# The last up product on modulated rows from its fifth block on

## Chip, cores and metric

One core of one Trainium2 chip runs the whole program. The metric is the device time of one execution in microseconds; the kernel before has a median of 1041.04 us over three runs.

## The reference

Two blocks of layers run one after the other on 256 rows (tokens) of 1024 numbers, all float32. The change is in the last layer's feed-forward part, which computes, with `x` the residual stream after the mixer:

```
h2 = rmsnorm(x, norm2_g) * (1 + sc2) + sh2      # sc2, sh2: one number per feature
x  = x + g2 * (square(relu(h2 @ w_ff1)) @ w_ff2)  # w_ff1 1024 x 4096, w_ff2 4096 x 1024
```

The rmsnorm's factor is one number per token (the reciprocal root of the mean square), `norm2_g`, `1 + sc2` and `sh2` are one number per feature.

## The kernel before

Float32 products run as three products of a split: each operand is its high part (rounded to the matmul's float32r form) plus the rest, and high x high, high x low and low x high are summed in PSUM. Weights come as units of 128x1024 through a ring of four (`raw`, loaded by SyncE's queue). ScalarE writes the high part of unit c (`wH`, line L1361, helper `hi`), VectorE the low part (`wL = raw - wH`, L2187, helper `lo`), and TensorE reads both. `ahead(i, U)` prepares the two units that are four further on, so units 8 and 9 (block 4's) are prepared at block 2. High parts are also counted against the ring: unit c waits until TensorE has finished unit c - 4. SyncE's queue loads unit c + 4 when the low part of unit c is done.

The last up product ("ff1") has 16 blocks. A block is 256 of the 4096 features, that is two units, each with 8 slices of the contraction and 3 products a slice, 48 products in all. Weights are the stationary operand, the tokens (256 columns) the moving one. Blocks 0 to 3 are written out, 4 to 15 are a loop of four-block bodies on TensorE.

Before, the product starts before the row factors are known. The moving operand is `nH`, `nL` (gain times the residual, not yet scaled by the row factor), and `nH` carries two more columns, the high and low part of the shift `sh2`, so the products with `nH` have 258 columns and those with `nL` 256. For each block VectorE then adds up the two shift columns (`shift_out`, L3124), multiplies the rest by the row factor `rcol` from PSUM into a staging buffer (L3126), and frees the bank; ScalarE applies relu with the shift as bias (L1990); VectorE squares into `act_a` (L3116). There are two staging buffers. The row factor comes from GpSimd (a power of -1/2, L2014), goes through two diagonal matrices by VectorE (`rd`, L2366) and one product by TensorE after block 1 (L626), and VectorE copies it to `rcol` (L2372) before it reads block 0. Up to there the finished blocks wait in PSUM.

The earlier feature-major products ("qkv", "up0", "up1", L606 to L608) have the same loop form with 256 columns and without shift columns. GpSimd fetches tiles of the modulation weights with DMAs (L2030, `mod_fetch`), weights some rows, and computes roots. Each engine works through its queue in the order written.

Of the kernel before, what the change touches and what calls it, by code (L numbers as in the profile page):

```python
# [15 lines left out]
F32 = mybir.dt.float32  # L16
F32R = mybir.dt.float32r
ALU = mybir.AluOpType
# [3 lines left out]
P = 128  # L22
SEQ = 256
# [124 lines left out]
PRODS = {"down0": 0, "down1": 22}  # L148
ACTS = {"down0": 0, "down1": 22, "ff2": 44}
AUX = 4  # L150

# [49 lines left out]
def turns(eng, count, body, steps=None, each=0, between=None, before_last=None):  # L203


    head = count % 4 or 4
    for j in range(head):
        body(0, j)
    if between:
        between()  # L210
    n = (count - head) // 4
    tail = 4 if n == 1 or before_last else 0
    n -= tail // 4
    if n > 0:
        with eng.Fori(0, n) as i:
            if steps is None:
                for j in range(4):
                    body(i, head + j)
            else:
                with steps.loop(i, n, 4 * each):  # L220
                    for j in range(4):
                        body(i, head + j)
    for j in range(count - tail, count) if count > head else ():
        if before_last and j == count - 1:
            before_last()
        body(0, j)
# [6 lines left out]
def build(nc, a, out):  # L233
    with ExitStack() as ctx:
# [3 lines left out]
        def sem(name):  # L238
            return ctx.enter_context(nc.semaphore(name))
# [35 lines left out]
        def place(kib, *names):  # L275

            with ExitStack() as s:
                if kib:
                    sb(f"pad_{names[0][0]}", [P, int(kib * 256)], where=s)
                return [sb(*n, where=s) for n in names]  # L280
# [25 lines left out]
        hf, = place(16, ("hf", [P, TT, D]))  # L306
        xvd, = place(48, ("xvd", [P, KD, SEQ]))
        nH, nL, shift_out = place(56.1875, ("nH", [P, KD, 320], F32R), ("nL", [P, KD, SEQ], F32R), ("shift_out", [P, 2, 2]))
        zL, = place(0, ("zL", [P, KD, SEQ], F32R))
        zH = yH  # L310

# [80 lines left out]
        half_done = sem("half_done")  # L392
        shift_hi = sem("shift_hi")
        relu_done = sem("relu_done")
        fin_rows = sem("fin_rows")
        fin_act = sem("fin_act")
        fin_pool = sem("fin_pool")
# [100 lines left out]
        def U(name):  # L498
            return 2 * BLOCKS[name][0]
# [101 lines left out]
        def _(pe):  # L601
# [706 lines left out]
            def shifted_up():  # L1308

                def weights(i, c):  # L1310
                    return [y.rearrange("p (k n) -> p k n", k=KD) for y in w_unit(i, 8, c)]

                def tile(o, w, k):
                    mm(o[:, 0:SEQ + 2], w[0][:, k], nH[:, k, 0:SEQ + 2], start=k == 0, stop=False, skip_group_check=True)  # L1314
                    mm(o[:, 0:SEQ], w[0][:, k], nL[:, k], start=False, stop=False, skip_group_check=True)  # L1315
                    return mm(o[:, 0:SEQ + 2], w[1][:, k], nH[:, k, 0:SEQ + 2], start=False, stop=k == KD - 1,  # L1316
                              skip_group_check=True)

                def body(i, j):
                    if j == 3:  # L1320
                        pe.wait_ge(r_done, r_order.index("ff1") + 1)
                    o = (bank("ff1", i, j), ps[AUX + (BANK["ff1"] + j) % 4])
                    if isinstance(i, int) and j == 0:
                        w = [weights(i, U("ff1") + f) for f in range(2)]
                        for k in range(KD):
                            if k == 3:
                                pe.wait_ge(unstaged, STAGED["wo_c"] + 4)
                                turn_pair(3, AUX + 3)
                            if k % 2 == 0:
                                pe.wait_ge(x_ready, READY["n2"] + k // 2 + 1)  # L1330
                            for f in range(2):
                                last = tile(o[f], w[f], k)
                                if k == KD - 1:
                                    last.then_inc(unit_done, 1)
                    else:
                        for f in range(2):
                            w = weights(i, U("ff1") + 2 * j + f)
                            for k in range(KD):
                                last = tile(o[f], w, k)
                            last.then_inc(unit_done, 1)  # L1340
                    if isinstance(i, int) and j == 1:
                        row_scale("ff1")
                turns(pe, BLOCKS["ff1"][1], body)
            mixer_out([zH, zL])
            shifted_up()
            down("ff2", FF2_TILES)
# [3 lines left out]
        def _(act):  # L1350
# [12 lines left out]
            def ahead(i, c):  # L1363

                hi(i, 8, c + SPLIT)
                hi(i, 8, c + SPLIT + 1)
# [46 lines left out]
            def projected(name):  # L1413

                def part(j):
                    act.wait_ge(unstaged, STAGED[name] + j + 1)
                    for t in range(TT):
                        c = slice(j * 256, (j + 1) * 256)
                        q = fn(hf[:, t, c], h[:, t, c], ACT.Square, accum_out=sqp[:, t, j:j + 1])
                        if j == 3:  # L1420
                            q.then_inc(sq_done, 1)

                def pair(b):
                    turned_pair("n2", "n2", b, AUX + b, lambda k: gs2[:, k:k + 1], nH[:, :, 0:SEQ])
                for j in range(4):
                    if j == 2:
                        part(0)
                        fn(nH[:, :, SEQ:SEQ + 1], modc[:, 24:32, 0].unsqueeze(2),
                           ACT.Copy).then_inc(shift_hi, 1)
                        pair(0)  # L1430
                    if j < 3:
                        act.wait_ge(unit_done, U(name) + OUT_DONE[j])
                        act.wait_ge(unstaged, STAGED[name] + j - 1)
                        fn(stage[:, (STAGED[name] + j) % 2].rearrange("p a b -> p (a b)"), ps[(BANK[name] + j) % 4][:],
                           ACT.Copy).then_inc(bank_free, 1)
                        ahead(0, U(name) + 2 * j)
                    else:
                        pair(1)
                        part(1)
                        part(2)  # L1440
                        ahead(0, U(name) + 2 * j)
                        pair(2)
                        pair(3)
                        part(3)
# [536 lines left out]

            win_act()
            projected("wo_c")
            def rectified(i, j):
                ahead(i, U("ff1") + 2 * j)
                n = STAGED["ff1"] + j
                act.wait_ge(bank_free, i * 4 + (BANK["ff1"] + j + 1))
                for f in range(2):
                    s = stage[:, n % 2, f]
                    last = fn(s, s, ACT.Relu, bias=shift_out[:, n % 2, f:f + 1])  # L1990
                last.then_inc(relu_done, 1)
# [20 lines left out]
        def _(pool):  # L2012
# [6 lines left out]
            def norm(n):  # L2019
                pool.wait_ge(ms_done, STAT[n] + 1)  # L2020
                inverse_root(rstd[:], msq[:]).then_inc(rstd_done, 1)
# [127 lines left out]
            pool.wait_ge(pw_in, 8)  # L2149
            inverse_root(st_r[:, 3, 4:8], st_r[:, 2, 4:8]).then_inc(pw_out, 1)  # L2150
            norm("n2")
            pool.wait_ge(m_o, RET_H)
            mod_fetch(64, MOD_TILES)
            gate_store(1)
# [13 lines left out]
        def _(dve):  # L2168
# [941 lines left out]
            ahead(0, U("ff1"))  # L3110
            row_scale("ff1")

            def square(i, j):
                dve.wait_ge(relu_done, i * 4 + (j + 1))
                s = stage[:, (STAGED["ff1"] + j) % 2]
                tt(act_a[:, bass.ds((i * 4 + j) * 2, 2)], s, s, ALU.mult).then_inc(unstaged, 1)  # L3116

            def up_scaled(i, j):
                n = STAGED["ff1"] + j
                dve.wait_ge(unit_done, i * 8 + (U("ff1") + 2 * j + 2))  # L3120
                dve.wait_ge(unstaged, i * 4 + (n - 1))
                b = [ps[x + (BANK["ff1"] + j) % 4] for x in (0, AUX)]
                for f in range(2):
                    nc.vector.tensor_reduce(shift_out[:, n % 2, f:f + 1], b[f][:, SEQ:SEQ + 2], AX, ALU.add)  # L3124
                for f in range(2):
                    last = tt(stage[:, n % 2, f], b[f][:, 0:SEQ], rcol[:], ALU.mult)  # L3126
                last.then_inc(bank_free, 1)
                if not (isinstance(i, int) and j == 0):
                    ahead(i, U("ff1") + 2 * j)
                    square(i, j - 1)  # L3130
            turns(dve, BLOCKS["ff1"][1], up_scaled, st, 0, before_last=first_tiles("ff2"))
            square(0, BLOCKS["ff1"][1] - 1)

# [112 lines left out]
```

## Time and profile before

| | |
|---|---|
| median of three runs | 1041.04 us (1038.68 to 1042.88) |
| span of the profiled execution | 1037.3 us |
| profiled execution's own time | not listed apart from its span |
| TensorE busy | 96% of the span |
| VectorE, ScalarE, GpSimd busy | 82%, 59%, 10% |
| last up product | 847 to 939 us of the span |

Rows give the start in us, the length in us, engine, line, operation, what is written and read, and a count; square brackets hold the engine's idle time ahead of the instruction and what ended it. TensorE's matmuls overlap, so the distance between starts is what counts there. A length of VectorE or GpSimd includes the time in which an instruction was held up after it was issued.

### The profile page before, as it was taken

The page shows a single profiled execution, that of the slowest core. Times are in us where ns is not written, and L with a number is a line of the kernel's source. Part 1 is how long each engine was busy: PE and PEld are TensorE (multiplying, and loading weights), DVE is VectorE, ACT ScalarE, POOL GpSimd, SP SyncE. Part 2 cuts the span into 40 slices and gives each one's busy share as a digit, 9 for nine tenths or more (in the row PEclk, how much of TensorE's full clock was granted, in tenths as well). Part 3 has the DMA queues.
Part 4 walks back from the last instruction along what each step waited for, and adds up shares of the span by engine and source line. Part 5 has one row for each costly group of instructions (what it writes and reads, how often), then busy time and mean ns, then how long its engine had stood idle before and what let it go on. Part 6 is the DMA issues. An engine that isn't in the chain of part 4 may idle for free.

```text
span 1037.3 us, 20795 instructions
## 1 busy us (share of the span) xinstructions
PE 998.8 (96%) x7662; PEld 926.7 (89%) x7662; DVE 848.9 (82%) x1566; ACT 608.4 (59%) x1056; POOL 102.2 (10%) x115
## 2 busy tenths in 40 slices
PE   6999999999999999999899999999998899999996
PEld 6999898999998889988899998898777799998884
DVE  5899978798889979887898999867788876668856
ACT  6687534666666464574676666456364565545443
POOL 1014522000000000001100001001200210000001
PEclk9999999999999999999999999999999999999998
DMA  9674323687776868837786657834412158766852
GB/s 290 178 223 135 103 64 101 204 228 219 222 210 218 287 175 256 278 100 262 252 237 197 186 185 251 283 95 130 152 62 82 41 152 245 193 188 219 278 152 115
DMA packets 216194, 193.09 MB, mean 186 GB/s; under 512 B 6032, under 2 KB 193568, under 8 KB 216000
## 3 DMA queue, kind: packets, MB, share of 16 engines
q1 hardware_dynamic: 206560, 158.09, 51.4%
q0 software_dynamic: 9136, 33.51, 9.5%
q8 instruction: 41, 0.67, 0.3%
q10 hardware_dynamic: 432, 0.61, 0.2%
q14 instruction: 25, 0.20, 0.1%
HBM read 191.14 MB, written 1.06 MB: 185 GB/s over the span
## 4 chain that ended last, share of the span: by engine, by line
PE 84%; DVE 8%; ACT 4%; DMA 2%; issue 1%; POOL 1%; POOLq 0%; ACTq 0%; DVEq 0%
PE ps L606 23%; PE ps L607 22%; PE ps L608 22%; PE ps L1315 3%; PE ps L1316 3%; PE ps L1314 3%; DVE wL L2187 2%; DMA modw<-in_w_mod_t 1%; PE ps L887 1%; PE ps L874 1%; ACT wH L1361 1%; PE ps L1144 1%; DVE cv L2209 1%; PE ps L829 1%; PE ps L783 1%
## 5 line engine op out<-in xcount | busy, mean ns | idle before, releaser
L1361 ACT ACTIVATE wH<-raw 128x1024 fp32r<-128x1024 f32 x298 | 312.9, 1061 | 254.9 <-PE ps L608 190.7
L2187 DVE TENSOR_TENSOR wL<-raw,wH 128x1024 fp32r<-128x1024 f32 x298 | 357.7, 1225 | 59.5 <-ACT wH L1361 58.8
L606 PE MATMUL ps<-yH,wH 128*128 128x256 f32 x704 | 195.7, 278 | 3.7 <-DVE wL L2187 3.6
L607 PE MATMUL ps<-yL,wH 128*128 128x256 f32 x704 | 194.5, 276 | 0.0
L608 PE MATMUL ps<-yH,wL 128*128 128x256 f32 x704 | 194.5, 276 | 0.0
L606 PEld LDWEIGHTS ps<-yH,wH 128*128 128x128 f32 x704 | 132.2, 188 | 4.7 <-DVE wL L2187 1.5
L607 PEld LDWEIGHTS ps<-yL,wH 128*128 128x128 f32 x704 | 132.2, 188 | 0.1
L608 PEld LDWEIGHTS ps<-yH,wL 128*128 128x128 f32 x704 | 132.2, 188 | 0.0
L606 PE MATMUL ps<-wH,aH 128*128 128x512 f32 (+1 forms) x308 | 119.4, 388 | 0.0
L608 PE MATMUL ps<-wH,aL 128*128 128x512 f32 (+1 forms) x308 | 119.0, 386 | 0.0
L607 PE MATMUL ps<-wL,aH 128*128 128x512 f32 (+1 forms) x308 | 119.0, 386 | 0.0
L606 PE MATMUL ps<-wH,xH 128*128 128x256 f32 (+1 forms) x304 | 94.2, 310 | 3.3 <-DVE xL L2187 2.3
L607 PE MATMUL ps<-wL,xH 128*128 128x256 f32 (+1 forms) x304 | 91.9, 302 | 0.0
L608 PE MATMUL ps<-wH,xL 128*128 128x256 f32 (+1 forms) x304 | 91.9, 302 | 0.0
L3038 DVE SCALAR_TENSOR_TENSOR cv<-stage,cols,cv 128x254 f32<-128x254 f32 (+1 forms) x176 | 73.1, 477 | 0.0
L1315 PE MATMUL ps<-nL,wH 128*128 128x256 f32 x256 | 72.5, 283 | 0.0
L606 PE MATMUL ps<-xH,wH 128*128 128x256 f32 x256 | 71.5, 279 | 1.0 <-DVE xL L2240 0.8
L1314 PE MATMUL ps<-nH,wH 128*128 128x258 f32 x256 | 72.3, 282 | 0.0
L2030 POOL DMA_DIRECT2D modw<-in_w_mod_t x48 | 26.4, 551 | 464.5 <-DVE modc L2209 406.4
L1316 PE MATMUL ps<-nH,wL 128*128 128x258 f32 x256 | 72.1, 282 | 0.0
L608 PE MATMUL ps<-xH,wL 128*128 128x256 f32 x256 | 70.9, 277 | 0.0
L607 PE MATMUL ps<-xL,wH 128*128 128x256 f32 x256 | 70.9, 277 | 0.0
(430 smaller groups left out, 2178.2 us busy)
## 6 DMA issues: line engine op xcount, KB each, us to landing
raw<-in_f_w_up SPq DMA_DIRECT2D x88, 512.0 KB, 4.9
raw<-in_w_ff SPq DMA_DIRECT2D x64, 512.0 KB, 4.5
modw<-in_w_mod_t POOLq DMA_DIRECT2D x48, 512.0 KB, 5.5
raw<-in_f_w_down SPq DMA_DIRECT2D x44, 512.0 KB, 4.6
raw<-in_a_w_in SPq DMA_DIRECT2D x32, 512.0 KB, 4.9
raw<-in_w_in SPq DMA_DIRECT2D x22, 512.0 KB, 4.3
raw<-in_w_kv SPq DMA_DIRECT2D x16, 512.0 KB, 5.2
raw<-in_a_w_out SPq DMA_DIRECT2D x8, 512.0 KB, 3.4
```

Source lines behind the costliest of these rows:

```text
L606: mm(o, l[0], r[0], start=first, stop=False, skip_group_check=check)
L607: mm(o, l[0], r[1], start=False, stop=False, skip_group_check=check)
L608: return mm(o, l[1], r[0], start=False, stop=last, skip_group_check=check)
L783: tr = nc.tensor.transpose(ps[first + k // 2][:, o:o + P], rows[:, t, k * P:(k + 1) * P], ident)
L829: last = mm(ps[AUX + g][:, x * P:(x + 1) * P], feat[:, 8 + h0 + x, t * P:(t + 1) * P], feat[:, f0 + h0 + x, t * P:(t + 1) * P], start=True ...
L1314: mm(o[:, 0:SEQ + 2], w[0][:, k], nH[:, k, 0:SEQ + 2], start=k == 0, stop=False, skip_group_check=True)
L1315: mm(o[:, 0:SEQ], w[0][:, k], nL[:, k], start=False, stop=False, skip_group_check=True)
L1316: return mm(o[:, 0:SEQ + 2], w[1][:, k], nH[:, k, 0:SEQ + 2], start=False, stop=k == KD - 1, skip_group_check=True)
L1361: fn(slot(wH, c), raw[:, c % RAW], ACT.Copy).then_inc(hi_done, 1)
L2030: pool.dma_start(mod_tile(m), a["w_mod_t"][m * P:(m + 1) * P, :]).then_inc(mod_in[m % MOD_RING], 16)
L2187: return tt(o, x, hi.bitcast(F32), ALU.subtract)
L3038: c = stt(o[:, d:], x[:, 0:SEQ - d], w, o[:, d:], ALU.mult, ALU.add)
```

## The change

From block 4 on (`SHIFTED_UP = 4`) the up product reads fully modulated rows `xH`, `xL` = norm2(x) scaled by row factor and gain, plus the shift. GpSimd adds `nH + nL` into `mt` (two instructions of 128x1024), multiplies by the row factor after `rcol` is there (two more), and its tile fetches follow behind. ScalarE adds the shift and rounds into `xH` (eight of 128x256) in its turn of block 2, between the high parts and relu 2. VectorE forms `xL` (eight of 128x256) behind square 1 in its turn of block 2. TensorE waits for both halves before the loop of blocks 4 to 15. In these blocks both units go into the two halves of one bank, ScalarE takes relu of the whole bank into the staging buffer ahead of its high parts, and VectorE only squares.

```diff
+SHIFTED_UP = 4
+        mt, = place(47.9375, ("mt", [P, KD, SEQ]))
 # TensorE
                 def body(i, j):
+                    if j >= SHIFTED_UP:
+                        modulated(i, j)
+                        return
...
+                def modulated(i, j):
+                    b = bank("ff1", i, j)
+                    for f in range(2):
+                        w = weights(i, U("ff1") + 2 * j + f)
+                        for k in range(KD):
+                            last = three(b[:, f * SEQ:(f + 1) * SEQ], [y[:, k] for y in w], [y[:, k] for y in X],
+                                         k == 0, k == KD - 1)
+                        last.then_inc(unit_done, 1)
+                turns(pe, BLOCKS["ff1"][1], body, between=lambda: pe.wait_ge(mt_ready, 2))
 # ScalarE
+            def modulated_hi():
+                for part in range(2):
+                    act.wait_ge(mt_rows, part + 1)
+                    for k in range(4 * part, 4 * part + 4):
+                        last = fn(xH[:, k], mt[:, k], ACT.Identity, bias=modc[:, 24 + k, 0:1])
+                    last.then_inc(mt_hi, 1)
             def rectified(i, j):
+                n = STAGED["ff1"] + j
+                if j >= SHIFTED_UP:
+                    act.wait_ge(unit_done, i * 8 + (U("ff1") + 2 * j + 2))
+                    act.wait_ge(unstaged, i * 4 + (n - 1))
+                    fn(stage[:, n % 2].rearrange("p a b -> p (a b)"), ps[(BANK["ff1"] + j) % 4][:],
+                       ACT.Relu).then_inc(bank_free, 1)
+                    ahead(i, U("ff1") + 2 * j)
+                    return
                 ahead(i, U("ff1") + 2 * j)
+                if j == 2:
+                    modulated_hi()
 # GpSimd, behind norm("n2") and ahead of mod_fetch(64, MOD_TILES)
+            for part in range(2):
+                c = slice(4 * part, 4 * part + 4)
+                pool.wait_ge(x_ready, READY["n2"] + 2 * part + 2)
+                ptt(mt[:, c], nH[:, c, 0:SEQ].bitcast(F32), nL[:, c].bitcast(F32), ALU.add).then_inc(mt_sum, 1)
+            pool.wait_ge(r_done, r_order.index("ff1") + 1)
+            for part in range(2):
+                c = slice(4 * part, 4 * part + 4)
+                pool.wait_ge(mt_sum, part + 1)
+                ptt(mt[:, c], mt[:, c], four_of(rcol), ALU.mult).then_inc(mt_rows, 1)
 # VectorE
+            def modulated_lo():
+                for part in range(2):
+                    dve.wait_ge(mt_hi, part + 1)
+                    for k in range(4 * part, 4 * part + 4):
+                        last = stt(xL[:, k], mt[:, k], modc[:, 24 + k, 0:1], xH[:, k].bitcast(F32), ALU.add, ALU.subtract)
+                    last.then_inc(mt_ready, 1)
             def square(i, j):
-                dve.wait_ge(relu_done, i * 4 + (j + 1))
+                if j < SHIFTED_UP:
+                    dve.wait_ge(relu_done, j + 1)
+                if j >= SHIFTED_UP - 1:
+                    dve.wait_ge(bank_free, i * 4 + (BANK["ff1"] + j + 1))
...
             def up_scaled(i, j):
                 n = STAGED["ff1"] + j
+                if j >= SHIFTED_UP:
+                    ahead(i, U("ff1") + 2 * j)
+                    square(i, j - 1)
+                    return
...
+                if j == 2:
+                    modulated_lo()
```

## Rows read from the trace of the kernel before

**Rows 1.** The page: span, busy shares, granted clock in 40 slices, chain by engine

```profile
span 1037.3 us, 20795 instructions
...
PE 998.8 (96%) x7662; PEld 926.7 (89%) x7662; DVE 848.9 (82%) x1566; ACT 608.4 (59%) x1056; POOL 102.2 (10%) x115
...
PEclk9999999999999999999999999999999999999998
...
PE 84%; DVE 8%; ACT 4%; DMA 2%; issue 1%; POOL 1%; POOLq 0%; ACTq 0%; DVEq 0%
```

**Rows 2.** Writers of PSUM by line, ns min/median/max, first and last start

```profile
L1314 PE MATMUL ps<-nH,wH x256: 278/283/470, 847.0 to 939.0; 128*128 128x258 f32 x128
```

**Rows 3.** Timeline of VectorE: its first read of finished blocks, both up products

```profile
542.39 0.69 DVE L3025 TENSOR_TENSOR stage<-ps,rd 128x512 f32<-128x512 f32 x1 [0.56 <-PE ps L608]
...
596.79 0.69 DVE L3025 TENSOR_TENSOR stage<-ps,rd 128x512 f32<-128x512 f32 x1 [0.57 <-PE ps L608]
...
871.07 0.23 DVE L3124 TENSOR_REDUCE shift_out<-ps 128x1 f32<-128x2 f32 x2 [1.34 <-PE ps L1316]
...
933.84 0.23 DVE L3124 TENSOR_REDUCE shift_out<-ps 128x1 f32<-128x2 f32 x2 [1.95 <-PE ps L1316]
```

**Rows 4.** Timeline of TensorE behind a stall of "qkv" and one of "up1"

```profile
15.62 0.39 PE L606 MATMUL ps<-xH,wH 128*128 128x256 f32 x1 [0.16 <-DVE wL L2187]
15.85 0.28 PE L607 MATMUL ps<-xL,wH 128*128 128x256 f32 x1
...
28.92 0.28 PE L607 MATMUL ps<-xL,wH 128*128 128x256 f32 x1
...
514.78 0.38 PE L606 MATMUL ps<-yH,wH 128*128 128x256 f32 x1 [1.33 <-DVE wL L2187]
```

**Rows 5.** Timeline of ScalarE and VectorE, 853 to 866 us

```profile
853.68 0.58 DVE L2366 TENSOR_SCALAR rd<-cst,rstd 128x128 f32<-128x128 f32 x2 [0.59 <-POOL rstd L2014]
854.29 2.36 DVE L2187 TENSOR_TENSOR wL<-raw,wH 128x1024 fp32r<-128x1024 f32 x2
859.63 0.42 DVE L2372 COPY rd<-ps 128x256 f32<-128x256 f32 x1 [2.98 <-PE ps L626]
...
861.02 0.91 ACT L1990 ACTIVATE stage<-stage,shift_out 128x256 f32<-128x256 f32 x2 [5.81 <-DVE stage L3126]
...
862.91 2.36 DVE L2187 TENSOR_TENSOR wL<-raw,wH 128x1024 fp32r<-128x1024 f32 x2 [1.13 <-ACT wH L1361]
```

**Rows 6.** Timeline of GpSimd: its longer instructions, the last root, the fetches

```profile
123.80 3.75 POOL L2089 TENSOR_TENSOR tok<-tok,sm 128x1024 f32<-128x1024 f32 x2 [10.57 <-DVE AT L2505]
127.51 5.64 POOL L2094 TENSOR_TENSOR zs<-zs,rows_a 128x1024 f32<-128x1024 f32 x2
151.02 2.02 POOL L2097 TENSOR_TENSOR tok<-tok,sm 128x1024 f32<-128x1024 f32 x1 [2.91 <-ACT tok L1538]
...
852.05 1.60 POOL L2014 TENSOR_TENSOR rstd<-msq,mhalf 128x2 f32<-128x2 f32 x1 [27.93 <-DVE msq L2360]
853.61 1.68 POOL L2030 DMA_DIRECT2D modw<-in_w_mod_t  x3
...
1023.18 1.29 POOL L2161 TENSOR_TENSOR hf<-h,rows_f 128x512 f32<-128x512 f32 x1 [16.53 <-DVE h L3143]
```

**Rows 7.** VectorE beside GpSimd (timeline), and its scalar-tensor-tensor by line

```profile
150.06 4.06 DVE L2187 TENSOR_TENSOR wL<-raw,wH 128x1024 fp32r<-128x1024 f32 x2
...
820.62 0.68 DVE L2829 TENSOR_TENSOR rope<-o_r 128x512 f32<-128x512 f32 x1
...
1022.34 0.69 DVE L3143 TENSOR_TENSOR h<-h,stage 128x512 f32<-128x512 f32 x1
...
1023.66 1.35 DVE L3143 TENSOR_TENSOR h<-h,stage 128x512 f32<-128x512 f32 x1
...
L3038 DVE SCALAR_TENSOR_TENSOR cv<-stage,cols,cv x176: 469/477/486, 208.2 to 623.2; 128x255 f32<-128x255 f32 x88, 128x254 f32<-128x254 f32 x88
```

**Rows 8.** Weight units, 846 to 875 us: DMA from issue to landing

```profile
DMA to landing us min/median/max: 4.1/4.8/8.8
```

More of the change, by code:

```diff
@@ L394, in build @@
         relu_done = sem("relu_done")
+        mt_sum = sem("mt_sum")
+        mt_rows = sem("mt_rows")
+        mt_hi = sem("mt_hi")
+        mt_ready = sem("mt_ready")
         fin_rows = sem("fin_rows")
@@ L1342, in body @@
                         row_scale("ff1")
-                turns(pe, BLOCKS["ff1"][1], body)
+                def modulated(i, j):
[7 more added lines that the diff above has]
+                turns(pe, BLOCKS["ff1"][1], body, between=lambda: pe.wait_ge(mt_ready, 2))
             mixer_out([zH, zL])
@@ L1983, in _ @@
             projected("wo_c")
-            def rectified(i, j):
+            def modulated_hi():
[4 more added lines that the diff above has]
+                    last.then_inc(mt_hi, 1)
+            def rectified(i, j):
+                n = STAGED["ff1"] + j
[6 more added lines that the diff above has]
+                    return
                 ahead(i, U("ff1") + 2 * j)
-                n = STAGED["ff1"] + j
+                if j == 2:
+                    modulated_hi()
                 act.wait_ge(bank_free, i * 4 + (BANK["ff1"] + j + 1))
```

## The prediction

> **What bounds the kernel now.** I read the busy shares first, then the chain of work that ended last, then the stretch of the last up product in order of time, and last every place where GpSimd ran beside VectorE. TensorE is busy 96% of the span at full clock (2.4 GHz throughout), and the chain lies on it for 84% [rows 1]. The last up product (16 blocks of 48 products, block 0 from 847.0 us) is such a stretch: no wait of TensorE shows between 847 and 939 us, its three product lines run without a break [rows 2]. So only two things can move the end: the time of a product in blocks 4 to 15, and a wait that TensorE gets. VectorE and ScalarE matter only where TensorE waits for them, and of that there is little room: in blocks 0 to 3 VectorE is the late one. It finishes the low part of block 3's first weights at 862.91 + 1.2 = 864.1 us, block 3 begins at about 865.2 (a block is 5.71 us, and block 3's end releases VectorE at 871.07) [rows 3, 5].
>
> **What a product costs.** VectorE's first read of each finished block marks the period: 871.07 to 933.84 us are eleven blocks, 5.71 us each, 118.9 ns a product (products of 258, 256 and 258 columns in turn) [rows 3]. The other feature-major up product, all 256 columns, has 542.39 to 596.79 us for ten blocks: 5.44 us, 113.3 ns [rows 3]. But 256 columns alone don't promise that: in the very first product of this form TensorE came out of a stall at 15.62 us, and from 15.85 to 28.92 it ran 111 products at 117.7 ns; after another stall, which ended at 514.78, came the very blocks that have the 5.44 us [rows 3, 4]. So there are two paces for the same product: the quick one would give 12 x (5.706 - 5.44) = 3.2 us, the slow one (117.7 ns, 5.65 us a block) 12 x 0.056 = 0.7 us. I take the quick one: it holds through the 54 us of a loop of the same form and length, the slow one through 13 us outside a loop; but block 4 will come out of a stall, so both stay in the range.
> The Trainium skill (TensorE: Matmul & The Clock Gate, step-by-step: what each phase is for) has one column streamed in each cycle, so that two columns fewer in 2 of 3 products would be worth 384 x 2 / 2.4 GHz = 0.3 us. By that rule the sum below would be +5.9 us. The rows differ: 118.9 ns are 285 cycles for 257 columns on average.
>
> **What is added, and where it lies.** Removed: VectorE's two small sums and two scalings (0.9 us a block) and ScalarE's two relus (0.9 us) in twelve blocks, replaced by one relu of 512 columns (no row has it; at most the 0.9 us of the two of 256) [rows 5]. In blocks 4 to 15 neither engine is on the path: per block ScalarE has 0.9 + 2.1 us, and its work ends 3.0 us after the block, the low parts of the weights at 4.2, the square at 4.9, all under 5.44. Worth nothing, cover 0.5 us; the weights' high part now waits for the block's end, which is hidden while block j + 2 is what they feed.
> Added on the path are the modulated rows: GpSimd two sums and two products of 128x1024, ScalarE eight 128x256, VectorE eight 128x256, and TensorE's wait for the last before block 4.
> *Prices.* GpSimd: 1.29 us for 128x512 with two full operands, so 2.6 us each (bounds: 1.9 us, a 128x1024 product by one number a row, and 2.8 us, one by a repeated row) [rows 6]. VectorE: a scalar-tensor-tensor is 0.48 us, back to back 0.39, so eight take 3.2 us [rows 7]. ScalarE: two 128x256 take 0.91, so eight 3.4 us [rows 5].
> *Contention.* The trace has GpSimd and VectorE holding each other up. A VectorE sum that takes 0.69 us took 1.35 when it began inside a GpSimd product (1023.18 to 1024.47), and two weight subtractions took 4.06 us in place of 2.35 around a 2.02 us GpSimd product [rows 5 to 7]. So an instruction of one with two SBUF inputs waits for the other's to end, and they take turns. I charge it so.
>
> **The chain of blocks 2 to 4, on the trace's clock.** GpSimd ends the root at 853.65, and the first sum follows at once (before, DMA issues stood there).
> 1. VectorE's diagonals (853.68) take turns with the sums: sum, diagonal, sum end at about 859.3; only then come the low parts of block 2's weights, which in the trace ran from 854.29: 859.3 to 860.5 and to 861.65. Block 2 wants its first at 859.4 and starts at 860.55: **+1.15 us**.
> 2. The row scale is copied behind them, at 862.0 in place of 860.05. GpSimd's two products run 862.05 to 867.15. VectorE's scalings read PSUM and one SBUF tile and pass. ScalarE: relu 863.0, high parts 863.8 to 865.8. VectorE's low part for block 3 is ready at 864.9, where the second product has just begun; it runs 867.15 to 868.35. Block 3 wants it at 866.25, starts at 868.4: **+2.15 us**.
> 3. VectorE's queue now is: low part 869.5, square 870.1, scalings of block 2 at 870.95, low parts 872.05 and 873.2, square 873.8, then the eight new ones to 876.95. ScalarE's eight are done at 871.8 (it held back relu 2, whose reader, the square, comes later still), so they cost nothing; the rows are VectorE's queue. Block 4 wants them at 868.4 + 5.7 = 874.1, starts at 877.0: **+2.9 us**.
> Sum: 6.2 us later into block 4, and nothing behind gives it back, since TensorE is the bound to the end. With 1.9 us a GpSimd instruction the same steps give 3.6, with 2.8 us 7.25. With no contention at all, 2.0 us are left: the eight new ones queued behind square 1 at 869.7 end at 872.9, block 4 wanted 870.9.
> Moved as well: GpSimd's three tile fetches go from 853.61 to 867.2 [rows 6]. Their readers are in the down product after 939 us, GpSimd's next step waits there anyway, and a weight transfer held up by them (unit 10 of the product, issued at 868.4, wanted by VectorE from 877.7) has 9 us against 4.8 in the median and 8.8 at worst [rows 8]. Nothing. TensorE's queue behind its new wait holds only its own products; the DMA queue's issues follow the low parts and shift with them.
> Net: +6.2 - 3.2 = **+3.0 us**. The profiled execution has a span of 1037.3 us [rows 1], 3.7 under the median of 1041.04, which I take to lie around it in both kernels: span 1040.3, time **1044.0 us** (+0.3%). Half a per cent, 5.2 us, is about what the timing can tell from no change.
>
> **Rivals.**
> - *Slow pace after the stall* (slower): block 4 starts from a wait and TensorE falls into the 117.7 ns pace and keeps it through the loop: 6.2 - 0.7 = +5.5, 1046.5 us, +0.53%. It decides from a pace of about 117 ns on. For it: the stretch from 15.62 us. Against: the one from 514.78, and the length of the quick stretch [rows 3, 4]. Chance 0.20.
> - *The time goes by columns alone* (slower): 118.9 ns for 257.3 columns on average leave 118.3 for 256, a gain of 0.35 us in all: 6.2 - 0.35 = +5.9, 1046.9 us. For it: it is what shortening a product does if the two paces have another cause; against: the 113.3 ns of the same shape. Chance 0.07. It is the rule of the Trainium skill's page named above.
> - *Little contention* (first sums before the weights, or shorter GpSimd instructions): delay 2.0 to 3.6, so 1039.8 to 1041.4 us, no change. For it: a VectorE product that took its plain 0.68 us at 820.62, in the midst of two GpSimd products [rows 7]. Against: the two disturbed rows above. Chance 0.22.
> - *Longer hold-up* (2.8 us and more a piece, or a turn lost): 7.25 - 3.2 = +4.1 at the quick pace, 1045.1; with the slow one 1047.6. Chance 0.11.
> - *The stage buffers become the bound*: ScalarE's relu of block j waits for the square of j - 2. At 4.9 of 5.44 us it doesn't; if each block lost 0.27 us, the gain would be gone: 1047.2. Chance 0.03.
> My forecast itself 0.37. A gain of over 5.2 us has no source: with no delay whatever it is 3.2 us, 1037.8.
>
> **Numbers.** Range 1039.5 to 1047.3 us: from no contention at the quick pace to the slow pace with the stall as worked out. The likeliest alone: 1042.5 to 1045.5. Slower by over 0.5% are most of the slow-pace cases and the last: 0.21. Faster by over 0.5%: 0.02. Same: 0.77.
>
> **What would show it.** VectorE's low part of block 2's weights after 859 us; waits of TensorE before blocks 2, 3 and 4 of about 1, 2 and 3 us, the last put down to VectorE's write of xL; GpSimd's products over by 867 us; the period of blocks 5 to 15 at 5.44 (or 5.65) us. I am wrong if GpSimd's four take turns otherwise with VectorE (then the waits differ), or if the new period is still 5.7 us.

## The result and the profile after

The changed kernel takes 1044.52 us in the median of 20 runs (1040.39 to 1050.41), the kernel before 1040.58 (20 runs, 1038.47 to 1046.74). The ratio is 1.0037, 95% interval 1.0022 to 1.0051: slower by 3.9 us (2.3 to 5.3). That is clear of the noise, but below the half per cent from which the prediction counts a change. Forecast were 1044.0 us and "same".

Page of the changed kernel: span, busy shares, granted clock in 40 slices.

```profile
span 1044.5 us, 20752 instructions
...
PE 1001.9 (96%) x7662; PEld 929.2 (89%) x7662; DVE 847.9 (81%) x1526; ACT 606.5 (58%) x1052; POOL 111.7 (11%) x119
...
PEclk9999989999999999999999999999999999999998
```

Set beside [rows 1], the span is 7.2 us longer, and 3.9 us of that are not the change: the last up product starts at 850.90 in place of 847.01 us, and none of the added instructions has run by then (a second execution of the same program, in experiment 7, starts it at 847.88). A stretch of short products at 129 to 155 us had a mean granted clock of 0.87 here and 0.93 before; the "8" in the row of the clock is that stretch. So from here on each trace is read from the start of its up product, and **its length to the first product of the down stage** is the measure: 92.34 us before (847.01 to 939.35), 96.09 after (850.90 to 946.99), +3.75 us. Behind it the kernels need 97.95 us before and 97.51 after. The timing of the whole says +3.9.

**The waits.** TensorE's waits in the changed kernel, 850 to 946 us (TensorE's line, the writer that it waited for: us in total, times, longest), and its products around the starts of blocks 2 and 3, in time:

```profile
PE ps L612 <- DVE xL L3161: 3.0, 1, 3.0
PE ps L1320 <- DVE wL L2230: 1.5, 1, 1.5
```
```profile
862.90 0.59 PE L632 MATMUL ps<-rd,cst 128*128 128x256 f32 x2
863.63 0.36 PE L1320 MATMUL ps<-nH,wH 128*128 128x258 f32 x1
...
869.31 0.28 PE L1322 MATMUL ps<-nH,wL 128*128 128x258 f32 x1
871.06 0.36 PE L1320 MATMUL ps<-nH,wH 128*128 128x258 f32 x1 [1.46 <-DVE wL L2230]
```

Before, TensorE had no such wait [rows 2]. Block 2 starts behind the two row-scale products (L632) and is too little late for the view of waits to list it. I count a delay from start to start, less what the same step takes without a wait: block 3 is +1.63 us late (1.75 less 0.12), block 4 +3.14 (876.74 to 880.00, 3.26 less 0.12). Block 2 is about +0.4 late: its second product starts 12.92 us behind the product's start, 12.54 before. That makes 5.2 us.

**Who made them.** GpSimd, then VectorE, then ScalarE of the changed kernel in order of time; a length includes the time in which an instruction was held up.

```profile
857.52 2.40 POOL L2189 TENSOR_TENSOR mt<-nH,nL 128x1024 f32<-128x1024 f32 x1
859.88 2.39 POOL L2189 TENSOR_TENSOR mt<-nH,nL 128x1024 f32<-128x1024 f32 x1
865.03 4.80 POOL L2194 TENSOR_TENSOR mt<-mt,rd 128x1024 f32<-128x1024 f32 x2 [2.77 <-DVE rd L2415]
869.74 1.69 POOL L2064 DMA_DIRECT2D modw<-in_w_mod_t  x3
```
```profile
857.58 2.42 DVE L2409 TENSOR_SCALAR rd<-cst,rstd 128x128 f32<-128x128 f32 x1 [0.59 <-POOL rstd L2048]
859.92 2.42 DVE L2409 TENSOR_SCALAR rd<-cst,rstd 128x128 f32<-128x128 f32 x1
...
865.13 0.74 DVE L3184 TENSOR_TENSOR stage<-ps,rd 128x256 f32<-128x256 f32 x2
...
867.80 4.25 DVE L2230 TENSOR_TENSOR wL<-raw,wH 128x1024 fp32r<-128x1024 f32 x2 [1.13 <-ACT wH L1378]
...
876.42 3.25 DVE L3161 SCALAR_TENSOR_TENSOR xL<-mt,modc,xH 128x256 fp32r<-128x256 f32 x8
```
```profile
871.31 3.30 ACT L2006 ACTIVATE xH<-mt,modc 128x256 fp32r<-128x256 f32 x8
...
878.35 1.06 ACT L1378 ACTIVATE wH<-raw 128x1024 fp32r<-128x1024 f32 x1 [2.95 <-DMA raw<-in_w_ff]
...
892.87 0.60 ACT L2014 ACTIVATE stage<-ps 128x512 f32<-128x512 f32 x1 [2.94 <-PE ps L614]
...
941.75 0.60 ACT L2014 ACTIVATE stage<-ps 128x512 f32<-128x512 f32 x1 [2.95 <-PE ps L614]
```

VectorE's two diagonals take 0.58 us together in [rows 5]. Here the first is issued 0.06 us behind GpSimd's first sum and ends 0.08 us behind its end; the second does the same with the second sum (ends at 862.34 and 862.27): one is held up by one sum, 4.8 us together. Its two low parts for block 3, 2.36 us in [rows 5], take 4.25: the first is issued at 867.80, while GpSimd's second product runs, the product ends at 869.83, and block 3 starts at 871.06. The scalings of block 0 (L3184), which read PSUM and one tile of SBUF, stand inside the first of GpSimd's two products and take their plain 0.74 us for two: they pass, as assumed. VectorE then goes through the queue that the prediction lists: low part, square, scalings, low parts, square, and the eight of L3161 to 879.67; block 4 starts at 880.00. ScalarE waits 2.95 us for weights at 878.35, and 0.76 once more at 880.17, where before it had 0.7 us of such waits in the whole product; TensorE doesn't wait for it. The relu of a whole bank (0.60 us) shows the period of the last blocks: 892.87 to 941.75 are nine, 5.43 us each, against 5.71 us [rows 3].

**What nobody had forecast.** TensorE behind the wait for `xL`, first each product, then four stretches of the same time (columns: us, busy time and count of PE, PEld, DVE, ACT, POOL, granted clock, DMA share, GB/s):

```profile
880.00 0.58 PE L612 MATMUL ps<-xH,wH 128*128 128x256 f32 x1 [2.98 <-DVE xL L3161]
880.38 0.41 PE L613 MATMUL ps<-xL,wH 128*128 128x256 f32 x1
...
883.15 0.40 PE L614 MATMUL ps<-xH,wL 128*128 128x256 f32 x1
...
883.98 0.28 PE L614 MATMUL ps<-xH,wL 128*128 128x256 f32 x1
884.09 0.28 PE L612 MATMUL ps<-xH,wH 128*128 128x256 f32 x1
```
```profile
874.00:879.00 5.00, 3.02 (x26) 2.81 (x24) 5.00 (x10) 2.05 (x5) 0.00 (x0) 1.00 1.09 342
879.00:881.00 2.00, 0.99 (x4) 1.00 (x5) 2.00 (x7) 1.24 (x2) 0.00 (x0) 0.75 1.20 292
881.00:883.00 2.00, 2.00 (x12) 2.00 (x11) 2.00 (x3) 1.02 (x3) 0.00 (x0) 0.50 1.14 276
...
890.00:946.00 56.00, 56.00 (x497) 56.00 (x496) 31.31 (x33) 26.18 (x34) 0.00 (x0) 1.00 0.67 189
```

The first products start 213 ns apart, from 883.5 on 113: TensorE came out of the wait at 1.2 GHz (clock 0.50) and ran 15 products so. From 880.00 to 883.51 it started 16 products, 3.51 us where 113.3 ns each make 1.81: 1.7 us lost. Of that 0.1 us is lost at full clock too (0.22 us from the first product to the second in experiments 3 and 5), so 1.6 us are the clock's. The terms close: 5.2 + 1.7 - 3.2 = +3.7 us, measured +3.75.

### The profile page after: what moved, and what is told of

The parts are those of the page before. It is cut to its first block, busy times and chain, and to the rows that moved or that the text cites. A ratio compares the mean times of both kernels' runs of the same rounds, so it can differ in the third digit from the quotient of the medians.

```text
span 1044.5 us, 20752 instructions
## 1 busy us (share of the span) xinstructions
PE 1001.9 (96%) x7662; PEld 929.2 (89%) x7662; DVE 847.9 (81%) x1526; ACT 606.5 (58%) x1052; POOL 111.7 (11%) x119
## 4 chain that ended last, share of the span: by engine, by line
PE 77%; DVE 13%; ACT 4%; DMA 2%; issue 2%; POOL 1%; POOLq 0%; ACTq 0%; DVEq 0%
PE ps L612 23%; PE ps L613 23%; PE ps L614 23%; DVE wL L2230 3%; DMA modw<-in_w_mod_t 2%; PE ps L893 1%; ACT wH L1378 1%; PE ps L1150 1%; DVE cv L2252 1%; PE ps L880 1%; PE ps L789 1%; PE ps L1000 1%; DVE cv L3031 1%; DVE st_p L2791 0%; DVE modw L2252 0%
## 5 line engine op out<-in xcount | busy, mean ns | idle before, releaser
L612 PE MATMUL ps<-xH,wH 128*128 128x256 f32 x448 | 126.6, 283 | 3.8 <-DVE xL L3161 3.0
L613 PE MATMUL ps<-xL,wH 128*128 128x256 f32 x448 | 126.0, 281 | 0.0
L614 PE MATMUL ps<-xH,wL 128*128 128x256 f32 x448 | 126.0, 281 | 0.0
L612 PEld LDWEIGHTS ps<-xH,wH 128*128 128x128 f32 x448 | 86.1, 192 | 4.5 <-issue 4.4
L614 PEld LDWEIGHTS ps<-xH,wL 128*128 128x128 f32 x448 | 86.1, 192 | 0.0
L613 PEld LDWEIGHTS ps<-xL,wH 128*128 128x128 f32 x448 | 85.8, 191 | 0.0
```

The lines of the kernel that those rows point to most:

```text
L612: mm(o, l[0], r[0], start=first, stop=False, skip_group_check=check)
L613: mm(o, l[0], r[1], start=False, stop=False, skip_group_check=check)
L614: return mm(o, l[1], r[0], start=False, stop=last, skip_group_check=check)
```

## The experiments

"Product" is the length defined above, in a trace of the kernel ("traced again" is a second execution of the same program, "fill" means idle products ahead of the wait); the timed ratio is to the kernel before, run beside it.

| kernel | product | against before | timed ratio, 95% interval | pace from block 4 on |
|---|---|---|---|---|
| before | 92.34 us | | | 118.9 ns |
| after | 96.09 | +3.75 | 1.0037, 1.0022 to 1.0051 | 113.3 |
| after, traced again | 97.35 | +5.01 | not timed | 113.3 |
| 256 columns alone | 89.13 | -3.21 | 0.9957, 0.9937 to 0.9977 | 113.3 |
| GpSimd's four alone | 94.40 | +2.06 | 1.0001, 0.9984 to 1.0019 | 118.8 |
| 24 products fill the wait | 94.50 | +2.16 | 1.0017, 0.9996 to 1.0037 | 113.3 |
| half of xL | 95.45 | +3.11 | 1.0001, 0.9981 to 1.0021 | 117.7 |
| half of xL, traced again | 95.46 | +3.12 | not timed | 117.8 |
| half of xL, 12 fill | 95.44 | +3.10 | not timed | 117.8 |
| all of xL, 12 fill | 97.05 | +4.71 | not timed | 117.7 |
| without the sums | 95.10 | +2.76 | 1.0052, 1.0027 to 1.0076 | 113.3 |
| without the sums, traced again | 95.15 | +2.81 | not timed | 113.3 |
| modulated rows from block 8 | 90.20 | -2.14 | 0.9975, 0.9955 to 0.9996 | 118.8, from block 8 on 113.3 |

The two measures don't agree everywhere. A product length is that of one execution and leaves out what lies ahead of the product and behind it; the start of the product alone lies between 846.2 and 856.4 us in the thirteen traces. For GpSimd's four alone (+0.20% by the product) and half of `xL` (+0.30%) the product's figure lies above the timed interval, and the kernel without sums (+0.27%) is timed at +0.52%. So the product lengths show what happens inside the product, and no more.

**1. The columns alone.** The kernel before, with products of 256 columns from block 4 on; the shift is left out there.

```diff
-    mm(o[:, 0:SEQ + 2], w[0][:, k], nH[:, k, 0:SEQ + 2], ...)
+    mm(o[:, 0:n], w[0][:, k], nH[:, k, 0:n], ...)        # both products with nH
-    last = tile(o[f], w, k)
+    last = tile(o[f], w, k, SEQ + 2 if j < 4 else SEQ)
```

> The kernel before with one part alone: blocks 4 to 15 read nH with 256 columns instead of 258, and the shift is left out of these blocks (no shift sums by VectorE there, and the relu's bias is an old one). Theory A, the two columns alone cost the 0.27 us a block: the period of blocks 5 to 15 is 5.44 us as in the changed kernel, 3.2 us less in all, ratio to before about 0.997. Rival, the place or stride of nH in SBUF is the cause and xH, xL are what helped: the period stays 5.7 us, and the time is that of before. Second rival, a product's time goes by its columns: 0.03 us a block, 0.35 us in all.

Measured: no wait of TensorE in the product, which takes 3.21 us less; the kernel is faster, 1037.33 us against 1040.71. VectorE's first reads of finished blocks, in time:

```profile
886.24 0.75 DVE L3126 TENSOR_TENSOR stage<-ps,rd 128x256 f32<-128x256 f32 x2 [1.80 <-PE ps L1316]
...
918.88 0.76 DVE L3126 TENSOR_TENSOR stage<-ps,rd 128x256 f32<-128x256 f32 x2 [1.81 <-PE ps L1316]
```

Six blocks in 32.64 us, 5.44 each. The two columns are what costs; neither the operand nor the bank that the products go to does. VectorE's small sums over the two columns are gone here as well, but they aren't it: in the kernel before, TensorE's products from 854.61 to 858.89 us are 118.9 ns apart, and the first such sum runs at 860.09.

**2. GpSimd's four alone.** The kernel before with GpSimd's sums and products, and nobody that reads `mt`.

```diff
+    ptt(mt[:, c], nH[:, c, 0:SEQ].bitcast(F32), nL[:, c].bitcast(F32), ALU.add).then_inc(mt_sum, 1)
...
+    ptt(mt[:, c], mt[:, c], four_of(rcol), ALU.mult).then_inc(mt_rows, 1)
```

> The kernel before plus GpSimd's four new instructions alone (their result is read by nobody; its tile fetches follow them as in the changed kernel). Theory A, they hold up VectorE: the diagonals and the low parts of block 2's weights come 4 us late, low parts of block 3's 2.4 us late, TensorE waits about 0.4 us before block 2 and 1.5 us before block 3, none before block 4 (there VectorE has caught up), clock full: +1.9 us, ratio about 1.002. Rival, the waits of blocks 2 and 3 come from the moved fetches or from chance: VectorE's lengths stay 1.22 and 0.29 us and no wait shows, ratio 1.000.

TensorE's waits, then VectorE's diagonals and its low parts for block 3:

```profile
PE ps L1317 <- DVE wL L2199: 1.6, 2, 1.4
```
```profile
854.57 4.77 DVE L2378 TENSOR_SCALAR rd<-cst,rstd 128x128 f32<-128x128 f32 x2 [0.59 <-POOL rstd L2017]
...
864.78 4.23 DVE L2199 TENSOR_TENSOR wL<-raw,wH 128x1024 fp32r<-128x1024 f32 x2 [1.13 <-ACT wH L1364]
```

The delays of blocks 2 and 3 are there to 0.02 us (gaps of 0.75 and 1.73 us against 0.73 and 1.75 in the changed kernel), 2.06 us in all, and the product has no other delay. They are GpSimd's hold on VectorE, with VectorE's lengths as in the changed kernel; the moved fetches, the rival, are issued only at 866.74 us, when GpSimd's products are over. In this execution TensorE waited another 0.9 us late in the down product, behind a weight transfer of 12 us; that lies outside the product. The timing (+0.2 us, interval -1.7 to +2.0) does not confirm the 2.06 us.

**3. The wait filled.** Ahead of its wait TensorE runs 24 idle products of block 4's first weights into the bank that block 4 then starts anew.

```diff
+    def filled():
+        b, w = bank("ff1", 0, 4), weights(0, U("ff1") + 8)
+        for n in range(24):
+            mm(b[:, 0:SEQ], w[0][:, n % KD], nH[:, n % KD, 0:SEQ], start=n == 0, stop=n == 23, ...)
+        pe.wait_ge(mt_ready, 2)
-    turns(pe, BLOCKS["ff1"][1], body, between=lambda: pe.wait_ge(mt_ready, 2))
+    turns(pe, BLOCKS["ff1"][1], body, between=filled)
```

> The changed kernel, and TensorE runs 24 idle products (256 columns, block 4's first weights with nH, overwritten by block 4) ahead of its wait for xL; the values are those of the changed kernel. They take 2.8 us and fit into the wait of 3.0 us. Theory A, the fall of the granted clock to 0.5 for 3.4 us behind the wait comes from TensorE's idling there: the clock stays 1.00, block 4 takes 5.4 instead of 7.4 us, the time from the start of the last up product to the end is 1.6 us shorter than in the changed kernel, ratio to before about 1.002. Rival, the fall comes from something else near 880 us (the burst of transfers at 342 GB/s, the power drawn): it stays, and block 4 still takes 7 us.

Its wait for `xL` and a stretch behind block 4's start (849.93 + 29.10 = 879.03 us):

```profile
PE ps L612 <- DVE xL L3168: 0.3, 1, 0.3
```
```profile
880.00:882.00 2.00, 2.00 (x20) 2.00 (x20) 2.00 (x3) 0.92 (x3) 0.00 (x0) 1.00 1.04 255
```

Block 4 starts as late as in the changed kernel (29.1 us behind the product's start in both), the clock stays at 1.00, and the product is 1.59 us shorter. That is the price of the clock, against 1.6 from the rows above. The rival, the burst of transfers, falls too: it is still there (255 GB/s in this row, where the changed kernel has 276 to 292).

**4. Half of xL.** Four of VectorE's eight instructions are left out; the other half of `xL` keeps old contents. It ran twice.

```diff
-                    for k in range(4 * part, 4 * part + 4):
+                    for k in range(4 * part, 4 * part + 2):
```

> The changed kernel with four of VectorE's eight instructions for xL left out (the other half of xL keeps old contents). Theory A, block 4 waits for VectorE's queue: the wait before block 4 falls by 1.6 us, from 3.0 to 1.4; whether the clock still falls behind a wait of 1.4 us is open (in the trace of before waits of up to 1.3 us at 514 us did not show a lower clock): if it stays, block 4 is another 1.6 us shorter, 3.2 us in all, ratio to before about 1.000. Rival, the wait is for ScalarE's rows or GpSimd's products: it stays at 3.0 us.

> The kernel with four of the eight xL instructions left out, unchanged, one more look. If kernel and waits fix the pace, it is the slow one again (95.4 us from the product's start to the down product, clock 1.00 throughout). If it is chance, the quick one may come: 93.0 us.

The wait for `xL`, and the relu of two blocks six apart (first kernel):

```profile
PE ps L612 <- DVE xL L3161: 1.4, 1, 1.4
```
```profile
885.40 0.60 ACT L2014 ACTIVATE stage<-ps 128x512 f32<-128x512 f32 x1 [3.15 <-PE ps L614]
...
919.32 0.60 ACT L2014 ACTIVATE stage<-ps 128x512 f32<-128x512 f32 x1 [3.16 <-PE ps L614]
```

The wait shrinks by what was left out and the clock stays at 1.00, but a block takes 33.92 / 6 = 5.65 us: the slow pace of the prediction's first rival, both times. What the clock and the shorter wait give (3.2 us), the pace takes back (12 x 0.21 = 2.5): the product is 0.64 us shorter than in the changed kernel. The timing, 1.0001, is what was expected with the quick pace; why it is lower than the product length says stays open.

**5. What chooses the pace?** Two kernels with 12 products ahead of the wait, with half and with all of `xL`.

```diff
-        for n in range(24):
+        for n in range(12):
```

> As the half-xL kernel (four of VectorE's eight left out, so half of xL holds old contents), with 12 idle products of block 4's first weights ahead of the wait, 12 x 113 ns = 1.4 us, which is all of that kernel's wait. It asks what chose the slow pace of 117.7 ns there. Theory A (an idle wait at full clock is what puts TensorE on the slow pace): no wait is left, so blocks 4 to 15 run at 113.3 ns (period 5.44 us) and the product takes 95.46 - 12 x 0.21 = 92.9 us. Rival B (it is the shorter VectorE work, or where block 4 starts against the other engines): the slow pace stays, 117.7 ns, and the product takes 95.4 us.

> The changed kernel with 12 instead of 24 idle products ahead of its wait: 1.4 us of the 3.0 are filled, 1.6 are left idle. Theory A (idle at full clock without a fall of the clock gives the slow pace): if the clock stays at 1.00, blocks 4 to 15 run at 117.7 ns and the product takes 94.5 + 12 x 0.21 = 97.0 us. If the clock falls for this wait too, 113.3 ns come back and 1.6 us and more are lost to the clock, about 96.1. Rival B (the pace has nothing to do with the wait): full clock and 113.3 ns, 94.5 us.

TensorE's waits, with half and with all of `xL`:

```profile
PE ps L1320 <- DVE wL L2237: 1.5, 1, 1.5
```
```profile
PE ps L1320 <- DVE wL L2237: 1.6, 2, 1.5
PE ps L612 <- DVE xL L3168: 1.6, 1, 1.6
```

The second met theory A (clock 1.00, 117.7 ns, 97.05 us against the 97.0 expected). The first refutes it: no wait is left ahead of block 4, and the slow pace is there all the same. The rival fell too: in the second kernel VectorE has all its work and block 4 starts where it does in experiment 3, which runs at 113.3. So neither an idle wait nor the moment of the start sets the pace by itself.

**6. Without the sums.** GpSimd's two sums are left out, so `xH` and `xL` are made from `nH` alone. It ran twice.

```diff
-    ptt(mt[:, c], nH[:, c, 0:SEQ].bitcast(F32), nL[:, c].bitcast(F32), ALU.add).then_inc(mt_sum, 1)
...
-    ptt(mt[:, c], mt[:, c], four_of(rcol), ALU.mult).then_inc(mt_rows, 1)
+    ptt(mt[:, c], nH[:, c, 0:SEQ].bitcast(F32), four_of(rcol), ALU.mult).then_inc(mt_rows, 1)
```

> The changed kernel with GpSimd's two sums left out: its two products multiply nH alone (the low half nL is left out of the modulated rows). Theory A, the sums alone delay the diagonals and block 2's weights and through them the row scale: low parts of block 2's weights back at 2.2 us behind the root, no wait before block 2; the row scale is 1.0 us earlier, the products too, so the wait before block 3 stays near 1.2 to 1.6 us (the low part still meets the second product) and that before block 4 near 3. Delay 0.4 to 0.8 us less than in the changed kernel. Rival: it is the number of GpSimd pieces that counts, then half of all delays goes.

> The kernel without GpSimd's two sums once more (xH and xL made from nH alone), since its times and its one trace disagree: 1046.1 us in the median, but a product of only 95.1 us, 1.0 less than in the changed kernel, in the execution that was also its fastest. If the product itself varies (a longer time at 1.2 GHz, as in the second look at the changed kernel, or the slow pace), a second trace shows a product of 96 to 97.6 us. If what varies lies ahead of the product, the product is again 95.1 and the execution's surplus stands ahead of it.

```profile
PE ps L612 <- DVE xL L3157: 3.2, 1, 3.2
PE ps L1320 <- DVE wL L2226: 0.9, 1, 0.9
```

Block 2 is on time, TensorE waits 0.9 us before block 3 and 3.2 us before block 4 (first execution), the clock falls to 0.50 again, and the product is 1.0 us shorter than in the changed kernel. Block 4 starts 28.34 us behind the product's start in place of 29.10: so 0.76 us of the 1.0 are delay that the sums had made, and the rest is a stretch at 1.2 GHz that was two products shorter. The timing disagrees: 1046.09 us over ten runs, while both traced executions (1041.58 and 1042.62 us) are among the fastest. They can't show what the others lose. The slowest traces of all (experiment 4's second and the kernel with all of `xL` and 12 ahead, spans of 1049.4 and 1048.0 us) have their surplus ahead of the product, which starts at 856.38 and 853.39 us, with a clock of 0.67 from 129 to 155 us; for this kernel no trace shows it.

**7. The changed kernel again.** The same program once more.

> The changed kernel unchanged, one more look at which pace TensorE takes behind the wait before block 4. If kernel and waits fix the pace, blocks 5 to 15 have 5.44 us again and the clock falls again behind a wait of 3.0 us. If it is chance from execution to execution, 5.65 us may come: the product is then 2.3 us longer (98.4 us from its start to the down product in place of 96.1).

The same gaps to 0.02 us, but TensorE stayed at 1.2 GHz for longer; two stretches behind the wait (it ended at 876.99 us), and one later:

```profile
878.00:880.00 2.00, 2.00 (x11) 2.00 (x11) 2.00 (x3) 0.91 (x3) 0.00 (x0) 0.50 1.06 258
880.00:882.00 2.00, 2.00 (x11) 2.00 (x11) 0.33 (x1) 0.00 (x0) 0.00 (x0) 0.50 0.79 221
...
884.00:886.00 2.00, 2.00 (x20) 2.00 (x19) 0.00 (x0) 0.32 (x1) 0.00 (x0) 1.00 0.04 11
```

The product takes 97.35 us, 1.26 more: behind the same wait the fall of the clock cost 1.6 us in one execution and 2.9 in another.

**8. A better version.** The modulated rows start with block 8, and their making is taken apart: each of GpSimd's four follows one of VectorE's squares, the rounding and `xL` come at block 5. More blocks are written out ahead of the loops (8 on TensorE, 12 on ScalarE and VectorE). It computes what the changed kernel computes.

```diff
-SHIFTED_UP = 4
+SHIFTED_UP = 8
+    pool.wait_ge(unstaged, STAGED["ff1"] + 2 * part + 1)     # ahead of each sum
+    pool.wait_ge(unstaged, STAGED["ff1"] + 2 * part + 2)     # ahead of each product
-                if j == 2:                                   # modulated_hi(), modulated_lo()
+                if j == 5:
```

> The changed kernel with the modulated rows from block 8 on and spread out: GpSimd sum and product of the first half, then of the second, each behind one of the squares 0 to 3, ScalarE's eight in turn 5, VectorE's eight behind square 4. Theory A: each GpSimd piece of 2.4 us falls into VectorE's slack, TensorE waits nowhere in the product, the clock stays at 1.00, blocks 8 to 15 have 5.44 us (if the switch comes without a stall the quick pace follows as in the kernel with 256 columns alone): the product is 8 x 0.27 = 2.1 us shorter than before, 90.2 us from its start to the down product in place of 92.3, ratio to before about 0.998. Rival, GpSimd's pieces delay low parts past their block wherever they stand: waits of 1 to 2 us show in blocks 3 to 6 and the time is that of before. With the slow pace in blocks 8 to 15 only 0.4 us are gained.

GpSimd's first, second and last piece, and VectorE's low parts beside the first:

```profile
870.89 2.39 POOL L2189 TENSOR_TENSOR mt<-nH,nL 128x1024 f32<-128x1024 f32 x1 [12.29 <-DVE act_a L3168]
876.25 2.44 POOL L2192 TENSOR_TENSOR mt<-mt,rd 128x1024 f32<-128x1024 f32 x1 [2.96 <-DVE act_a L3168]
...
886.95 2.43 POOL L2192 TENSOR_TENSOR mt<-mt,rd 128x1024 f32<-128x1024 f32 x1 [2.96 <-DVE act_a L3168]
```
```profile
871.72 3.78 DVE L2228 TENSOR_TENSOR wL<-raw,wH 128x1024 fp32r<-128x1024 f32 x2
```

The low parts are still held up (3.78 us for 2.35), but end ahead of the block that wants them. TensorE waits for nothing in the product, the clock stays at 1.00, the pace is quick from block 8 on: -2.14 us, where 8 x 0.266 is -2.13. With 1038.95 us against 1041.20 it beats the kernel before; its interval, 0.04% to 0.45% faster, excludes no change, if barely. The changed kernel was not timed beside it, but its ratio, 1.0037, lies well above this one.

## Why the prediction came out right

1044.0 was forecast, 1044.52 measured; as a change, +3.0 was forecast and +3.9 measured. By its own steps:

- **The quick pace, -3.2 us: right.** Experiment 1 gives -3.21 with nothing else changed on TensorE, and the changed kernel runs at 113.3 ns.
- **Block 2, +1.15 us forecast, about +0.4 measured: mis-sized.** The turns came as charged, one diagonal with each sum, but GpSimd's instructions take 2.4 us in place of 2.6, and the diagonals add next to nothing: the second ends 0.07 us behind the second sum. They end 4.8 us behind the root and not 5.65.
- **Block 3, +2.15 forecast, +1.63 measured.** The mechanism is right to the instruction: the low part waits for the end of the second product. But the copy of the row scale, which lets the products begin, came 0.9 us earlier (with the sums), and the two took 4.8 us against 5.1, while block 2 was only 0.7 us earlier than forecast. So the step shrank from 2.15 to 1.63.
- **Block 4, +2.9 forecast, +3.14 measured.** The queue of VectorE ran as listed, and the eight took 3.25 us against 3.2 assumed. In all, 6.2 us were forecast for the three and 5.2 measured; experiment 2 shows 2.06 of it to be GpSimd's.
- **The clock, nothing forecast, +1.6 measured.** The step that failed is the first: full clock throughout [rows 1], carried over to a stage that was being given a wait of 3 us. The slow pace was weighed as what a stall can leave behind, a fall to 1.2 GHz was in no term and no rival. Experiment 3 shows its price by taking it away (1.59 us), and experiment 7 that it can be 2.9.
- **ScalarE's eight and GpSimd's moved fetches, nothing: not contradicted.** The eight end at 874.6, ahead of VectorE's; no wait of TensorE or VectorE leads to a fetch. ScalarE did wait up to 2.95 us for weights there, which cost TensorE nothing; whether the fetches delayed them is not shown.

So the total is right by luck as well as by mechanism. Two misses, -1.0 and +1.6 us, partly cancel; they leave the change 0.7 to 0.9 us larger than forecast, and the median of before, 1040.58 here against the 1041.04 from which the forecast started, takes 0.46 us of that out of the total again. In the second execution, with its 2.9 us for the clock, the product is +5.0 us, 2 above the forecast.

The rival of the slow pace (+5.5) did not happen in the changed kernel, but did in four traces of three kernels next to it: its chance of 0.20 was not idle. Columns alone (+5.9) is refuted by experiment 1: two columns in two of three products cost 5.6 ns a product, 13 cycles. The Trainium skill (TensorE: Matmul & The Clock Gate, step-by-step: what each phase is for) has one column a cycle, so 1.3 cycles a product here; the measurement decides. Little contention is refuted by the held-up instructions of experiment 2, longer hold-up by GpSimd's 2.4 us a piece, stage buffers as the bound by the steady 5.43 us.

**What stays open:** what chooses between 113.3 and 117.7 ns behind the start of block 4. Each kernel kept its pace from there over the whole loop, and the three that ran twice had the same one again, which speaks against chance but, with three pairs, doesn't exclude it; the idle wait, VectorE's load and the time of the start are each excluded alone by experiment 5. Why the kernel without sums is timed slower than its traces, and GpSimd's four alone and half of `xL` faster than theirs, isn't settled either, nor is what makes the stretch at 1.2 GHz longer in one execution than in another.

## What to carry to other kernels

Price the wait that an edit brings not only by its length: ask what TensorE does when it comes out of it, as the clock took back 1.6 and 2.9 us here, and the slow pace 2.5. Work put on GpSimd isn't beside VectorE's but in turns with it where both read tiles in SBUF, so it belongs where VectorE is idle anyway: the same four instructions cost 2.06 us in one lump at the tightest place and nothing when spread behind the squares. A saving per block can be had later and for fewer blocks, if that takes its preparation off the path: eight blocks without a wait (-2.1 us) are worth more than twelve behind one (+3.75).

## What the runs showed of the hardware

- The clock: 1.2 GHz behind waits of 3.0 to 3.2 us (four traces), where it stayed for about 3 to 6 us; 2.4 GHz throughout behind waits of 1.4 and 1.6 us (three traces), and where 24 products left 0.3 us idle. The Trainium skill (TensorE: Matmul & The Clock Gate, Part 1) has the clock halved behind idle time. The four traces agree, and the engine's idle time is what experiment 3 removed.
- The pace of 128x256 products, weights loaded for each, was one of two at full clock in these traces, 113.3 or 117.7 ns (272 or 283 cycles), and was kept through a loop of 65 us.
- VectorE's scaling by a number a row (`rd`, 128x128) has one full operand, in SBUF, and is held up by GpSimd just as the subtractions with two are: two of them took 0.58 us before and 4.8 here, each ending just behind one sum of GpSimd. The scalings from PSUM passed at 0.74 us for two. The Trainium skill (SBUF — State Buffer, Who interferes with whom) has VectorE's instructions with two SBUF inputs, or in a two-port mode, and GpSimd's exclude each other, and the one that is issued later wait for the other's whole length. The trace agrees for the subtractions (2.36 us became 4.25); that the scaling is in a two-port mode no run here shows.
- GpSimd takes 2.4 us for 128x1024 with two full operands, 2.38 to 2.44 us a piece over all runs, product or sum alike.
